# A two-block kernel on one core: scan inputs kept in SBUF, pooling moved to the projection's tail, weights and context loaded a stage ahead

## What is computed

```python
h_lat = modulate(rms_norm(x, g1), ...); h_ctx = modulate(rms_norm(ctx, g1), ...)
p = split(h @ w_in, IN_SPLITS)   # pool 256, z 384, x-B-C 896, dt 12, qkv 1152, gate 384, a 12, b 12
# pool: mean over windows of 2, 4, 8, 16 tokens minus the token, times a 64 x 64 block per group, times a scale
# ssd ("the scan"): silu(conv5(xbc)); a decayed state in both directions, context first; y * silu(z); rms_norm
# gdn ("the delta rule"): silu(conv5(qkv)) in column-major order; chunks of 64; rms_norm; times silu(gate)
lat = concatenate([pool(p0), s_lat, g_lat]) @ w_out
x = x + m2 * lat
x = x + m5 * expert_choice_ffn(modulate(rms_norm(x, g2), ...))      # 16 experts, hidden width 512
out = rms_norm(x, final_g)
```

## Time and profile before

| | |
|---|---|
| Median of 3 runs | 4182.35 us (4179.74 to 4183.69) |
| The profiled execution | 4178.34 us, its span 4176.5 us |
| TensorE busy | 3721.6 us, 89% of the span |
| VectorE, ScalarE, GpSimd busy | 1521.8, 699.6, 479.6 us |
| Mean granted TensorE clock | 0.949 of 2.4 GHz |
| Moved by DMA | 816.18 MB |
| Projection stage | 2558.1 to 2995.3 us of the span |
| Scan, both stages | 2995.3 to 3154.2 |
| Delta rule: preparation, steps, tail | 3154.2 to 3225.5 to 3540.6 to 3584.0 |
| Output projection with routing | from 3584.0 |

### The profile page before, as it was taken

The page is one execution under the profiler, slowest core; times in us unless marked ns, Lnnn a source line. Parts: engine busy times, 40 slices in busy tenths (PEclk is TensorE's granted clock), DMA queues, the critical chain, the costliest instruction groups (busy, mean ns, idle before and its releaser), DMA issues. The chain is left out here.

```text
span 4176.5 us, 48152 instructions
## 1 busy us (share of the span) xinstructions
PE 3721.6 (89%) x19742; PEld 2087.2 (50%) x19742; DVE 1521.8 (36%) x2606; ACT 699.6 (17%) x1496; POOL 479.6 (11%) x529
## 2 busy tenths in 40 slices
PE   4999989997779999999999997999775997768995
PEld 2444468884334444444444444544453887334442
DVE  4565369992820000000000004452084777240003
ACT  1000012221101000100001002321135443011111
POOL 0000000002200000000000001000031874200110
PEclk8999999998889999999999998999887999889997
DMA  6556332224278898889888885221202000219995
GB/s 267 197 222 256 156 121 101 110 82 188 81 297 317 308 311 305 312 306 310 306 309 310 299 306 185 104 89 61 104 1 76 4 4 33 110 61 363 340 332 175
DMA packets 287549, 816.18 MB, mean 195 GB/s; under 512 B 15088, under 2 KB 22312, under 8 KB 272132
## 3 DMA queue, kind: packets, MB, share of 16 engines
q1 hardware_dynamic: 267080, 720.76, 47.8%
q0 software_dynamic: 19168, 82.08, 6.0%
q10 hardware_dynamic: 1116, 10.71, 0.6%
HBM read 718.86 MB, written 94.66 MB: 195 GB/s over the span
## 5 line engine op out<-in xcount | busy, mean ns | idle before, releaser
L1289 PE MATMUL banks<-moe_ring,moe_xeT 128*128 128x512 f32 x2560 | 1129.1, 594 | 7.3 <-ACT moe_xeT L1330 7.3
L1289 PEld LDWEIGHTS banks<-moe_ring,moe_xeT 128*128 128x128 f32 x2560 | 481.7, 191 | 584.4 <-issue 581.6
L1383 DVE TENSOR_TENSOR moe_hid<-moe_silu,banks 128x512 f32<-128x512 f32 x80 | 55.0, 688 | 1428.0 <-PE banks L1289 1428.0
L1275 PE MATMUL banks<-moe_ring,moe_hidT 128*128 128x512 f32 x1280 | 562.6, 592 | 1.7 <-DVE moe_ye L1369 1.0
L1275 PEld LDWEIGHTS banks<-moe_ring,moe_hidT 128*128 128x128 f32 x1280 | 240.8, 190 | 293.4 <-issue 291.3
L1598 PE MATMUL banks<-hT,w_in_ring 128*128 128x512 f32 (+3 forms) x976 | 362.3, 533 | 1.7 <-ACT hT L1670 0.9
L434 PE MATMUL banks<-hT,w_in_ring 128*128 128x512 f32 x768 | 343.0, 601 | 3.2 <-ACT hT L456 3.2
L1598 PEld LDWEIGHTS banks<-hT,w_in_ring 128*128 128x128 f32 (+1 forms) x976 | 181.9, 187 | 180.2 <-issue 170.3
L1349 ACT ACTIVATE moe_silu<-banks 128x512 f32<-128x512 f32 x80 | 47.8, 597 | 1302.4 <-PE banks L1289 1302.4
L434 PEld LDWEIGHTS banks<-hT,w_in_ring 128*128 128x128 f32 x768 | 143.7, 191 | 194.0 <-issue 181.1
L973 PE MATMUL banks<-w_out,mix 128*128 128x512 f32 x512 | 221.8, 596 | 7.4 <-DMA w_out<-d_w_out 7.4
(11 more groups left out here) (425 smaller groups left out, 3942.0 us busy)
## 6 DMA issues: line engine op xcount, KB each, us to landing
moe_ring<-d_wg SPq DMA_DIRECT2D x80, 2048.0 KB, 9.6
moe_ring<-d_wu SPq DMA_DIRECT2D x80, 2048.0 KB, 8.2
moe_ring<-d_wd SPq DMA_DIRECT2D x80, 2048.0 KB, 8.0
x_normed<-d_ada_w SPq DMA_DIRECT2D x12, 2048.0 KB, 11.9
w_in_ring<-d_w_in SPq DMA_DIRECT2D x9, 2048.0 KB, 10.6
x_normed<-d_mod_w SPq DMA_DIRECT2D x8, 2048.0 KB, 15.2
d_taps<-dft SPq DMA_DIRECT2D x8, 2048.0 KB, 7.4
taps_in<-d_taps SPq DMA_DIRECT2D x8, 2048.0 KB, 9.4
```

The lines of the kernel that those rows point to most:

```text
L1275: last = nc.tensor.matmul(m.ps[:, Y_BANK + h, :], hidT[:, c, i * P:(i + 1) * P], down(c)[:, i, h * BANK:(h + 1) * BANK], start=(fc == 0 an ...
L1289: last = nc.tensor.matmul(m.ps[:, 2 * kind + c, :], xeT[:, k, :], up(c, kind)[:, k, :], start=(k == 0), stop=(k == KT - 1))
L1383: nc.vector.tensor_tensor(hid[:, j % 2, :], sg[:, j % 2, :], m.ps[:, 2 + j % 2, :], ALU.mult).then_inc(s.hid, 1)
```

## The change

What it does, place by place:

- The last scatter of the first expert stage is awaited by the next stage's SyncE instead of by GpSimd. In that expert stage SyncE also loads the context behind the first turn, VectorE and ScalarE normalise it behind their first turn, and SyncE loads the first two chunks of `w_in2` behind its last expert weights.
- The projection stage keeps x-B-C in `ssd_chan`, silu(z) in the upper part of `m.X`, the small rows in `small_out`, all in SBUF; only q, k, v and the gate go to `chan`. The constants of the scan are loaded there. The pooling is done at the stage's end on VectorE, its products stand on TensorE between the latent units and z, and ScalarE writes them where the output projection reads them (`m.mixT` is now `m.X`).
- The scan's stages have no transfer of their own left; the delta rule's first products read `small_out` directly.
- `w_out2` is loaded while the delta rule's steps run. The delta rule's tail has no pooling, and works in two halves.

```diff
+def context_ahead(nc, m, s):
+    ctx, mom, mv, rstd = m.ctx, m.ctx_mom, m.ctx_mv, m.ctx_rstd
+    def on_sync(sp):
+        sp.dma_start(ctx[:], m.dram["ctx"]).then_inc(m.ahead.ctx, 16)
+    def on_vector(v):
+        v.wait_ge(m.ahead.ctx, 16)
+        for t in range(CT):
+            for h in range(2):
+                nc.vector.bn_stats(mom[:, t, h, :], ctx[:, t, h * BANK:(h + 1) * BANK]).then_inc(s.ctx_stat, 1)
...
+        v.wait_ge(s.ctx_std, 1)
+        nc.vector.reciprocal(rstd[:], rstd[:]).then_inc(s.ctx_stat, 1)
...
+            nc.vector.tensor_scalar(ctx[:, t, :], ctx[:, t, :], rstd[:, t:t + 1], None, ALU.mult).then_inc(s.ctx_xh, 1)
+    def on_scalar(act):
+        act.wait_ge(s.ctx_var, 1)
+        nc.scalar.activation(rstd[:], rstd[:], ACT.Sqrt).then_inc(s.ctx_std, 1)
...
+def load_input_weights(sp, m, q):
+    cols = input_weights(q)
+    sp.dma_start(m.w_in2[:, q % 2, :, 0:cols.stop - cols.start], m.dram["w_in2"][:, :, cols]
+                 ).then_inc((m.ahead.w0, m.ahead.w1)[q % 2], 16)
...
 # experts_stage
             load(0)
+            if before_next:
+                ctx_sp(sp)
             load(1)
             with sp.Fori(2, TURNS) as turn:
                 load(turn)
             load_down(d_down[E - 1], FU - 1, E * nf - 1)
+            if before_next:
+                for q in range(2):
+                    load_input_weights(sp, m, q)
+                sp.wait_ge(m.ahead.ctx, 16)
+                for sem in (m.ahead.w0, m.ahead.w1):
+                    sp.wait_ge(sem, 16)
...
-            pool.wait_ge(s.scattered, 16 * E)
+            if before_next:
+                m.scattered = s.scattered
+            else:
+                pool.wait_ge(s.scattered, 16 * E)
...
 # mixer_in_stage
-            sp.dma_start(ctx[:], m.dram["ctx"]).then_inc(s.ctx, 16)
+            sp.wait_ge(m.scattered, 16 * E)
             for t in range(TT):
                 sp.dma_start(m.X[:, t, :], m.dram["acc"][t * P:(t + 1) * P, :]).then_inc(arrived[t], 16)
-                if t in (1, 3):
-                    weights(t // 2)
+            sp.dma_start(pw[:], m.dram["pool_w"]).then_inc(s.pool_in, 16)
+            sp.wait_ge(s.tr_mm, KT)
+            sp.dma_start(inv[:], m.dram["pool_inv"]).then_inc(s.pool_in, 16)
+            sp.dma_start(m.ssd.tri[:], m.dram["tri"]).then_inc(s.ssd_in, 16)
+            sp.dma_start(m.ssd.rows[:], m.dram["ssd_rows"].partition_broadcast(P)).then_inc(s.ssd_in, 16)
+            sp.dma_start(m.ssd.steps[:], m.dram["ssd_steps"].partition_broadcast(P)).then_inc(s.ssd_in, 16)
             for q in range(2, N_CHUNKS):
-                weights(q)
+                sp.wait_ge(s.p_mm, chunk_done(q - 2))
+                load_input_weights(sp, m, q)
             sp.wait_ge(s.p_mm, chunk_done(N_CHUNKS - 2))
             sp.dma_start(wz, m.dram["w_z"]).then_inc(s.wz, 16)
+            sp.wait_ge(s.ssd_in, 48)
...
-            pool.wait_ge(s.small, 5)
-            pool.dma_start(m.dram["small"], small[:]).then_inc(s.small_out, 16)
-            for t in range(TT):
-                pool.wait_ge(s.z_read, t + 1)
-                pool.dma_start(m.dram["z"][:, t, :], ob[:, t % 2, 0:SSD_W]).then_inc(z_stored[t % 2], 16)
...
-            pe.wait_ge(s.ctx_xh, CT)
...
+            pe.wait_ge(s.pool_in, 32)
+            pe.wait_ge(s.diff, 1)
+            for n in range(2 * POOL_T):
+                i, h = n // 2, n % 2
+                if n >= 2:
+                    pe.wait_ge(s.pool_out, n - 1)
+                nc.tensor.matmul(m.ps[:, 6 + n % 2, :], pw[:, i, :], diff[:, i, h * BANK:(h + 1) * BANK], start=True, stop=True
+                                 ).then_inc(s.pool_mm, 1)
             pe.wait_ge(s.wz, 16)
...
-                nc.scalar.activation(ob[:, t % 2, 0:SSD_W], m.ps[:, 6 + t % 2, 0:SSD_W], ACT.Silu).then_inc(s.z_read, 1)
+                nc.scalar.activation(sz[:, t, :], m.ps[:, 6 + t % 2, 0:SSD_W], ACT.Silu).then_inc(s.z_read, 1)
...
-            v.wait_ge(s.ctx, 16)
-            for t in range(CT):
-                squares(TT + t, ctx[:, t, :])
...
+            v.wait_ge(s.p_read, group_of(CONV_T + POOL_T - 1, 2))
+            st.link(nc.vector.tensor_tensor(psum[:, :, 0, 1:L], pr[:, :, 0:L - 1], pr[:, :, 1:L], ALU.add))
+            st.link(nc.vector.tensor_tensor(psum[:, :, 1, 2:L - 1], psum[:, :, 0, 1:L - 2], psum[:, :, 0, 3:L], ALU.add))
+            v.wait_ge(s.pool_in, 32)
+            st.did(nc.vector.tensor_tensor(diff[0:64, 0, :], psum[0:64, 0, 0, body], inv[0:64, 0, :], ALU.mult))
...
+            nc.vector.tensor_tensor(diff, diff, pr[:, :, body], ALU.subtract).then_inc(s.diff, 1)
...
 # ssd_prep_stage: all six loads and the waits for them go
-            sp.dma_start(t.chan[:], m.dram["chan"][0:XBC_T].rearrange("i p t -> p i t")).then_inc(s.chan, 16)
-            sp.dma_start(dtr[:], m.dram["small"][0:2 * SSD_H, :]).then_inc(s.small, 16)
...
-            act.wait_ge(s.rows, 64)
...
 # gdn_prep_stage
-            for to, at, n in parts:
-                act.dma_start(ab[:, to:to + n], m.dram["small"][32:SMALL, at:at + n]).then_inc(s.steps_in, 16)
...
-            pe.wait_ge(s.steps_in, 64)
...
 # gdn_stage
+        @block.sync
+        def _(sp):
+            load_projection(sp, m, m.dram["w_out2"])
...
 # gdn_out_stage: PARTS = 2, NC = LAT_CHUNKS // PARTS; pooling, its loads and its products go
+            for h in range(PARTS):
+                pe.wait_ge(s.normed, h + 1)
+                for p in range(PAIRS):
+                    for c in range(NC):
+                        for half in HALVES:
+                            last = nc.tensor.matmul(m.ps[half, 2 * p + h, c * CHUNK:(c + 1) * CHUNK], t.out[half, h * NC + c, p, :],
+                                                    t.tab[half, EYE, :], start=True, stop=True)
+                    last.then_inc(s.tr_mm, 1)
...
+            mean_square(0)
+            scaled(0)
+            mean_square(1)
+            scaled(1)
...
 # mixer_out_stage
-            if not deep:
-                load_projection(sp, m, m.dram["w_out2"])
```

296 lines of the change are left out of this document (145 added, 151 removed).

## The result

The changed kernel takes 4107.19 us (median of 4 runs, 4105.56 to 4108.79), the kernel before 4182.64 (one run more than in the table above, 4179.74 to 4183.69): a ratio of 0.9825, 95% interval 0.9812 to 0.9837, so 75.5 us less where 77.4 were forecast. Repeated later it took 4109.02 (4103.91 to 4112.18, ratio 0.9828, interval 0.9814 to 0.9841). The profiled execution took 4106.33 us with a span of 4104.7, that is 71.8 us less span than before.

The account below looks back on a forecast made before the run. Products back to back bound most of the kernel; the change targets five TensorE holes ending with DRAM data or DRAM-delayed work. 15.3 + 21.3 + 1.0 + 5.8 + 26.6 + 7.4 = 77.4 us off 4182.35 gives 4105, range 4092 to 4128.

Parts of the forecast that it names:

- Place 1: Opening of the projection, context side and input weights: latent products start earlier, gain 15.3 us, bounds 9.8 to 20.1.
- so the stage can open at 2550.4: Projection stage: without GpSimd's wait for the last scatter it opens at 2550.4 instead of 2558.12.
- context products starting about 20 us earlier: Projection opening: sign that the forecast is right, counted relative to the last expert product.
- the first is there at 2561.5, where VectorE now begins: Projection opening: first x tile lands 3.9 us after the scatter; VectorE starts on it 9.0 us earlier than 2570.50.
- a wait of some 5 us of TensorE for scaled x: Before the latent transposes: sign that the forecast is right, TensorE ready at 2596.6, fourth tile scaled at 2601.4.
- Place 2: Projection tail to the scan's exponential: inputs stay in SBUF, pooling moves there; gain 21.3 us, bounds 19.8 and 22.1.
- The clock extra of 1.0 us: Scan's first fifty transposes: may run at 2.4 GHz with TensorE busy up to the boundary; 1.0 taken, 4 at most.
- Place 3: Delta-rule inputs: decay products no longer wait for small rows and steps; gain 5.8 us, at worst 4.
- Rival C: Delta-rule steps lengthen as VectorE and GpSimd fall into a worse phase: 83 us lost, 4188; chance 0.03.
- Place 4: Tail of the delta rule, without pooling and in halves: gain 26.6 us, between 22 and 29.
- Place 5: Output projection's weights already there: TensorE's 7.41 us of idling go; gain 7.4 us, at least 5.
- Rival A: Stage openings: holes covered code fetching, first instructions 5 to 8 us late at four places, about 4131; chance 0.10.

Follow-up runs that it names:

- ln_ahead: The changed kernel with the two rows of the layer norm loaded already in the expert stage, three of that stage's tiles moved to make room: 4106.24 us.
- warm_gate: The changed kernel with ten added TensorE products nobody reads, six behind the delta rule's last transposes, four at the output projection's opening: 4109.73 us.
- w_out2_late: The changed kernel with the second output projection's weights loaded in their own stage again: 4117.60 us, ratio 0.9854 to the kernel before.
- pool_gpsimd: The changed kernel with the pooling of the projection's tail on GpSimd instead of VectorE: 4103.75 us, ratio 0.9822 to the kernel before.
- no_last_scatter: The changed kernel without the scatter of the last expert's rows, so the output leaves out that expert's part: 4103.38 us (2 runs).

## Why the prediction was right, point by point

*Place 1: wrong in two steps, 4 us too high.* The first: "so the stage can open at 2550.4". It opened 5.9 us later (2554.83, and 1.5 for the earlier start of this execution), as the outstanding scatter holds the block's end; hence the sign "context products starting about 20 us earlier" showed as 14.2 us. The second: "the first is there at 2561.5, where VectorE now begins". VectorE's first instruction waits also for the layer norm's rows, 1 MB issued at the opening, and began 9.1 us behind the opening, 3.9 us later than forecast; ln_ahead puts their cost at 3.2 us. The second may follow from the first: rows issued at 2550.4 and as slow as here would have been there at 2559.5, before x. That is an estimate from the 9.1 us; no run tests it.

Some of what came out near was luck. "The landing stays at about 2558" takes the end of the wait for the landing; the list of DMA issues has it at 2555.0 in the kernel before. So the loads of x began 1.7 us earlier than forecast (2556.3), the first tile took 5.1 us (ln_ahead) instead of 3.9, and the sum, 2561.4, met the forecast 2561.5. The Trainium skill, "DMA: Bandwidth & Descriptors", section "Anatomy of one DMA", gives its fit for transfers that GpSimd issues, and these were SyncE's; the estimate of 3.2 us by it was 1.9 us under the measured 5.1. Nor was VectorE "nearly gapless": from its first instruction on x to the fourth scaled tile it took 39.9 us before and 37.0 after, which gave 2.9 us back. So the fourth tile came only 1.0 us later than forecast; TensorE, at half clock, came to it 2.9 us later than forecast, without a wait, and lost 1.2 us more behind the first group of transposes: 4.1 us in all. The sign "a wait of some 5 us of TensorE for scaled x" did not show in the first trace; in the second it is 2.57 us, before the second group of transposes.

*Place 2: right.* 20.9 us against 21.3; pool products 4.47 against 4.2; VectorE pooled from 2880.20 in 14.4 us against 14 (its elements by the rate of a pass), 40 us before its use.

*The clock extra of 1.0 us: not there.* From the exponential to the first product of states it was 16.70 us before, 16.29 after and 17.00 in the repetition. The first ten transposes ran at full clock (1.31 us), but TensorE then waited 3.08 us for ScalarE and went on at half clock: 20 transposes in 4.08 us, the next ten in 1.43 (the lines at L1932 above). From the opening of the stage TensorE did nothing but transposes, and the granted clock rose from 0.53 (2986.3 to 2988.3) over 0.62 to 1.00 (2990.4 to 2993.5). The same is in the kernel before, where the earlier trace rows end just ahead of it: 0.50 from 3022 to 3024, 0.79 to 3026, 1.00 to 3027.7, with transposes alone. At the opening of the projection the sixteen context transposes, at 0.50 to 0.62, were followed by products at full clock from the first in nine of eleven executions, in the other two by 3.5 us at 0.50. The Trainium skill, "TensorE: Matmul & The Clock Gate", section "Part 4: PE-mode transpose", says that transposes don't count as busy time for the clock in the way products do; for these float32 transposes the rise from 0.50 to 1.00 among them speaks against it, and the prediction's "the 5.00 us at 0.51 agrees" rested on a stretch that ended before the rise.

*Place 3: right,* 5.9 us (12.03 to 6.12 from ScalarE's last scan instruction to VectorE's first on the decay products) against 5.8.

*The delta rule: no loss, as said.* Rival C did not happen; its 1.1 us is in the scatter shown below.

*Place 4: right,* 26.4 against 26.6, and by its parts: the squares of both halves 2.86 us, a sum 1.75 and a scaling 1.76 for each half, turning 7.31, gates 6.04.

*Place 5: 5.8 and 1.1 against 7.4.* The weights' wait went in full, but two clock effects stood around it. The gate product lost 1.8 us, as it now follows 4.87 us of idling and not the pool products (warm_gate gives the 1.8 back); the output products gained 1.1, as they no longer follow 7.41 us of idling (w_out2_late loses 2.3 there).

*The sum.* The span shrank by 71.8 us where 77.4 were forecast, and 1.5 of it lie ahead of the change. That 4105 was so near 4107.19 is luck to some 3.5 us, in the step from the profiled execution to the median: before, the profiled run lay 4.3 us below the median of 4182.64, after, only 0.9. Rival A (late first instructions) did not happen: behind the other boundaries engines start within 0.3 to 0.8 us, and the one long gap with no releaser but the sequencer, 9.27 us at the first opening, is the scatter's.

## What to carry to other kernels

When several waits at a boundary are cleared, list every transfer that the next engine's first instruction needs, the small parameters too: the missed one is what ends last. TensorE going without a stop doesn't prove it the bound; look at the granted clock, since half clock can hide the wait that a second execution shows. Work whose inputs are there goes best right behind the last products of the stage before, where the clock is still full.

## What the runs showed of the hardware that was not expected

A scatter that GpSimd has issued holds the end of its block until 1.6 us after its landing, with no wait in the program (ten executions, landings 5.9 to 6.5 us after the issue).

The delta rule's time varies from run to run. Over twelve executions of kernels whose code there is the same, from VectorE's first instruction to the last attention product took 373.6 to 380.4 us, and it goes with TensorE's clock: seven with a mean of 0.96 or 0.97 from 3400 to 3490 us took 376.4 or less, five with 0.94 or less took 375.8 or more. The busy time of TensorE over 90 us (columns as above), in the shortest, pool_gpsimd:

```profile
3400.00:3490.00 90.00, 76.60 (x2348) 0.96 0.02 4
```

and in the longest, no_last_scatter:

```profile
3400.00:3490.00 90.00, 77.02 (x2210) 0.91 0.02 4
```

In the one the mean clock was 0.96, in the other 0.91. The stretch from the exponential of the step rates to the delta rule varies too, from 140.8 to 144.5 us. A few us of difference between two kernels' medians can come from there; what a small change is worth is better read from the stretch that it touches. Why the clock falls there in one execution and not in the next stays open.
